# Expert stage: the third low part moves from Pool to VectorE, the output copy from VectorE to ACT

## The chip, the cores and the metric

The kernel runs on one core of a Trainium2 chip. The metric is device time in microseconds (us) of one execution. Three runs of the kernel before took 919.23, 915.85 and 917.68 us, median 917.68. The engines are TensorE (PE in the rows; its weight loads are PEld), VectorE (DVE), ScalarE (ACT), GpSimd (POOL) and SyncE (SP, here used only to issue transfers; its queue is SPq). They work side by side, each through its own instructions in order, and wait for each other by semaphores.

## What is computed

One encoder layer on 768 tokens of width 1024 (512 of one sequence, 256 of another), in float32. First a mixer (attention branches with a gated sum), then a mixture of experts, then a last norm. The change touches only the experts:

```python
for e in range(N_EXPERTS):                       # 16 experts, D_EXPERT = 256
    he = jax.nn.silu(t @ w_exp_gate[e]) * (t @ w_exp_up[e])
    out = out + dense_w[:, e:e + 1] * (he @ w_exp_down[e]).astype(jnp.float32)
```

`dense_w` is nonzero for two experts of a token: it picks one of four groups, and the best two of the four experts in it.

## The kernel before, in words

Matmuls in full precision are made as three passes of rounded operands. Every operand is split into a high part (a copy rounded to the matmul's type) and a low part (the rest, operand minus high part); a product is high x high, high x low, low x high. So each expert weight goes through SBUF three times: raw as loaded, high, low.

The tokens are sorted by expert into tiles of 128 rows. In this execution there are 19 tiles, numbered from 0; three of them (13, 15 and 17) belong to the same expert as the tile before, so that 16 sets of weights are loaded. A set is three chunks of 128x2048 floats, 1024 KB each: chunk 0 (gate), 1 (up) and 2 (down). Raw chunks, high parts and low parts have two buffers each, by the tile's parity.

TensorE sets the order. For tile j it does, in `tile`: `turn_rows(j+1)`, eight transposes of the next tile's gathered rows; `gate_up(j)`, 24 matmuls; `down(j-1)`, 12 matmuls; `turn_hidden(j)`, two transposes of the hidden values. In the rows, L1102 is turn_rows, L1122 turn_hidden, and L831 to L833 are the three passes.

Around it, for tile j:

- SP loads the chunks 0 and 1 of tile j+4 and chunk 2 of tile j+3 (line 561) and stores the result of a finished tile (line 579). A raw buffer is loaded again when the low part of the tile two before it is made (`s_elo`).
- ACT makes the high parts: of the next rows (`xt_hi`, line 1396), the gate's tanh (1403), chunks 0 and 1 of tile j+2 (1318), the hidden values (`he_hi`, 1410), chunk 2 of tile j+1 (1318 again).
- DVE makes the low parts: of the next rows (`xt_lo`, 1818), the hidden product `he` in two steps (1828, 1830), chunks 0 and 1 of tile j+2 (1639); then it copies the output of tile j-1 out of PSUM (`y_sb`, 1843) and makes the hidden low part (`he_lo`, 1834).
- POOL gathers the rows of a tile from memory by an indirect transfer (724; inside the loop a small copy, 721, brings the indices ahead of it) and makes the low part of chunk 2 (733 and 739; 744 where the expert is the same as before).

Where a tile's expert is that of the tile before, the high and low parts are copied from the other buffer and nothing is loaded; a register and two branches decide that on each engine. Tiles 0 to 2 are written out; a hardware loop does two tiles in a round, and the last two are written out again.

Before the tiles start, SP issues chunk 2 of tiles 2 and 3 in this order, each of which waits for the low part of chunk 2 two tiles before it:

```python
            for j in (2, 3):
                load_expert(j, 0, j, 2)
            sp.wait_ge(s_fill, 16)
```

After this come chunks 0 and 1 of tile 4, and then the loop.

Of the kernel before, what the change touches and what calls it, by code (L numbers as in the profile page):

```python
# [28 lines left out]
ACT = mybir.ActivationFunctionType  # L29
ALU = mybir.AluOpType  # L30
AX = mybir.AxisListType

P = 128
# [23 lines left out]
SET = 3  # L57
# [152 lines left out]
def build(nc, x_prompt, x_sample, rel_bias, norm_mix, w_in, lam_q1, lam_k1, lam_q2, lam_k2, subln_g,  # L210
# [9 lines left out]
    with ctx:  # L220
# [8 lines left out]
        ones = misc("ones", [P, P])  # L229
# [79 lines left out]
        y_sb = at("y_sb", [P, 2, D], F32, A_OA + 24576)  # L309
# [168 lines left out]
        def over(ap, shape, dim):  # L478

            return ap.unsqueeze(dim).broadcast_to(shape)  # L480
# [14 lines left out]
        def late(r, j, first):  # L495

            return not isinstance(r, int) or j >= first

        def is_new(eng, r, j):

            return eng.value_load(regs[0:1, 2, bass.ds(r * 2 + j, 1)], min_val=0, max_val=1)
# [156 lines left out]
        def _(gp):  # L658
# [65 lines left out]
                gp.indirect_dma_start(xg[:, j % 2, :], None, h2_dram.ap(),  # L724
                                      bass.IndirectOffsetOnAxis(ap=ids, axis=0)).then_inc(s_xg[j % 2], 16)

            def split_lo_part(r, j, c):

                lo, hi = e_lo[j % 2][c], e_hi[j % 2][c]
                if not late(r, j, SET + 1):  # L730
                    gp.wait_ge(s_elo[c], r * 2 + j)
                    gp.wait_ge(s_ehi[c], r * 2 + (j + 1))
                    gp.tensor_tensor(lo, e_raw[j % 2][:, c, :], hi, ALU.subtract).then_inc(s_elo[c], 1)
                    return
                new = is_new(gp, r, j)
                with gp.If(new > 0):
                    gp.wait_ge(s_elo[c], r * 2 + j)
                    gp.wait_ge(s_ehi[c], r * 2 + (j + 1))
                    gp.tensor_tensor(lo, e_raw[j % 2][:, c, :], hi, ALU.subtract).then_inc(s_elo[c], 1)
                with gp.If(new < 1):  # L740
                    gp.wait_ge(s_elo[c], r * 2 + j)
                    gp.wait_ge(s_ehi[c], r * 2 + (j + 1))

                    gp.tensor_tensor(lo.rearrange("p (a b) -> p a b", b=P),
                                     e_lo[1 - j % 2][c].rearrange("p (a b) -> p a b", b=P),
                                     over(ones[:, :], [P, 16, P], 1), ALU.mult).then_inc(s_elo[c], 1)


            gp.wait_ge(s_tab, 1)
            for done in s_h2out:  # L750
                gp.wait_ge(done, 16 * (NT // 2))
            for j in range(3):
                gather(0, j)
            split_lo_part(0, 1, 2)

            loops = loop_count(gp)
            for j in (3, 4):
                gather(0, j)
            split_lo_part(0, 2, 2)
            with gp.Fori(0, loops) as r:  # L760
                for j in (3, 4):
                    gather(r, j + 2)
                    split_lo_part(r, j, 2)
            split_lo_part(loops, 3, 2)
            split_lo_part(loops, 4, 2)

            gp.wait_ge(s_ystored, 2)
            for t in range(NT):
# [391 lines left out]
        def _(act):  # L1160
# [141 lines left out]
            def split_expert(r, j, chunks):  # L1302

                par = j % 2
                new = is_new(act, r, j) if late(r, j, SET + 1) else None

                def free(c):


                    if c == 2 and late(r, j, 2):  # L1310
                        act.wait_ge(s_dn, r * 2 + (j - 1))

                def split(c):
                    free(c)
                    if late(r, j, SET + 1):
                        act.wait_ge(s_ehi[c], r * 2 + j)
                    act.wait_ge(s_eraw[c][par], r * 16 + 16 * (j // 2 + 1))
                    act.activation(e_hi[par][c], e_raw[par][:, c, :], ACT.Copy).then_inc(s_ehi[c], 1)  # L1318

                if not late(r, j, SET + 1):  # L1320
                    for c in chunks:
                        split(c)
                    return
                with act.If(new > 0):
                    for c in chunks:
                        split(c)
                with act.If(new < 1):
                    for c in chunks:
                        free(c)
                        act.wait_ge(s_ehi[c], r * 2 + j)  # L1330
                        act.activation(e_hi[par][c], e_hi[1 - par][c], ACT.Copy).then_inc(s_ehi[c], 1)
# [67 lines left out]
            def tanh_gate(r, j):  # L1399
                act.wait_ge(s_gu, r * 2 + (j + 1))  # L1400
                if late(r, j, 2):
                    act.wait_ge(s_he, r * 4 + 2 * (j - 1))
                act.activation(tanh_g[:, j % 2, :], main[0][:, 512 * (j % 2):512 * (j % 2) + DE], ACT.Tanh,
                               scale=0.5).then_inc(s_tanh, 1)

            def hidden_hi(r, j):
                act.wait_ge(s_htr, r * 2 + (j + 1))
                if late(r, j, 2):
                    act.wait_ge(s_dn, r * 2 + (j - 1))
                act.activation(he_hi[:, j % 2, :, :], work[1][:, 0:DE].rearrange("p (k n) -> p k n", k=2),  # L1410
                               ACT.Copy).then_inc(s_hehi, 1)

            def tile(r, j):
                rows_hi(r, j + 1)
                tanh_gate(r, j)

                split_expert(r, j + 2, (0, 1))
                hidden_hi(r, j)
                if late(r, j, 1):
                    split_expert(r, j + 1, (2,))  # L1420
# [7 lines left out]
                tile(r, 4)  # L1428
            rows_hi(loops, 4)
            tanh_gate(loops, 3)  # L1430
            hidden_hi(loops, 3)
            split_expert(loops, 4, (2,))
            tanh_gate(loops, 4)
            hidden_hi(loops, 4)

            for t in range(NT):
                act.wait_ge(s_comb, combined(t))
# [13 lines left out]
        def _(dve):  # L1451
# [380 lines left out]
            def hidden_lo(r, j):  # L1832
                dve.wait_ge(s_hehi, r * 2 + (j + 1))
                dve.tensor_tensor(he_lo[:, j % 2, :, :], work[1][:, 0:DE].rearrange("p (k n) -> p k n", k=2),
                                  he_hi[:, j % 2, :, :], ALU.subtract).then_inc(s_helo, 1)

            def copy_y(r, j):
                dve.wait_ge(s_dn, r * 2 + (j + 1))
                if not late(r, j, 1):
                    dve.wait_ge(s_fill, 16)  # L1840
                if late(r, j, 2):
                    dve.wait_ge(s_yout[j % 2], r * 16 + 16 * (j // 2))
                dve.tensor_copy(y_sb[:, j % 2, :], main[1][:, :]).then_inc(s_y, 1)

            def tile(r, j):
                rows_lo(r, j + 1)
                if not late(r, j, 1):
                    route_weights()
                hidden(r, j)
                split_expert(r, j + 2, (0, 1))  # L1850
                if late(r, j, 1):
                    copy_y(r, j - 1)
                hidden_lo(r, j)

            split_expert(0, 1, (0, 1))
            rows_lo(0, 0)
# [6 lines left out]
                tile(r, 4)  # L1863
            rows_lo(loops, 4)
            hidden(loops, 3)
            copy_y(loops, 2)
            hidden_lo(loops, 3)
            hidden(loops, 4)
            copy_y(loops, 3)
            hidden_lo(loops, 4)  # L1870
            copy_y(loops, 4)


            def finish(t):
# [82 lines left out]
```

## Time and profile before

| | before |
|---|---|
| median of 3 runs | 917.68 us (915.85 to 919.23) |
| profiled execution | 918.5 us, its span 916.7 us |
| PE busy | 842.0 us (92%) |
| DVE busy | 465.3 us (51%) |
| ACT busy | 392.3 us (43%) |
| POOL busy | 191.2 us (21%) |
| granted TensorE clock over the span | 0.972 of full speed |

The expert stage lies at about 680 to 876 us of the span. Busy shares over the whole span hide it, since the mixer before it uses the engines otherwise. A row of the timeline gives an instruction's start, its duration, its engine and line, and in brackets how long the engine had stood idle before it and what ended that. Starts can lie some 0.1 us before the end of the instruction ahead, as engines overlap them.

### The profile page before, as it was taken

The numbers are of one execution on the slowest core, as the hardware profiler recorded it, in microseconds if no ns is written. First come the engines' busy times: TensorE is split into PE (matmuls) and PEld (weight loads), VectorE is DVE, ScalarE is ACT, GpSimd is POOL, SyncE is SP. The second block draws the span as 40 slices with busy tenths as digits, with TensorE's granted clock in tenths as the row PEclk, the third lists the DMA queues.
The fourth block names the chain that finished last, engine by engine and source line by source line (L and its number), as shares of the span: only waits on it lengthen the run. The fifth ranks groups of instructions, "written<-read, shape, count | busy, mean of one in ns | idle before, by whom it ended". The sixth has DMA issues, their size and how long they took to land.

```text
span 916.7 us, 13495 instructions
## 1 busy us (share of the span) xinstructions
PE 842.0 (92%) x5122; PEld 719.6 (79%) x5122; DVE 465.3 (51%) x760; ACT 392.3 (43%) x540; POOL 191.2 (21%) x132
## 2 busy tenths in 40 slices
PE   3999999999999999999999999999989998989910
PEld 3988888998788888888888888888977876878700
DVE  4511354454419632333233147434598877777537
ACT  5522244444432543334333202234426866767413
POOL 0001010000000001100100001300024778767553
PEclk9999999999999999999999999999899999999965
DMA  9315131322121314321311114873869999988675
GB/s 290 88 56 122 47 75 46 76 67 55 36 76 34 93 46 75 87 58 46 76 47 46 46 46 154 244 324 129 308 207 324 370 375 381 390 284 276 230 278 207
DMA packets 97355, 142.46 MB, mean 155 GB/s; under 512 B 4567, under 2 KB 75431, under 8 KB 97223
## 3 DMA queue, kind: packets, MB, share of 16 engines
q1 hardware_dynamic: 89368, 115.05, 37.2%
q0 software_dynamic: 7904, 26.44, 10.6%
q8 instruction: 36, 0.59, 0.3%
q10 hardware_dynamic: 32, 0.26, 0.3%
q14 instruction: 15, 0.11, 0.0%
HBM read 116.31 MB, written 25.43 MB: 155 GB/s over the span
## 4 chain that ended last, share of the span: by engine, by line
PE 77%; DVE 7%; SPq 6%; DMA 4%; issue 3%; ACT 2%; POOL 1%; ACTq 0%; DVEq 0%; POOLq 0%
PE main L831 20%; PE main L833 19%; PE main L832 19%; PE work L910 3%; SPq L579 3%; PE work L880 2%; PE work L943 2%; PE work L927 2%; PE work L1071 1%; SPq L561 1%; PE work L1049 1%; DVE x L1891 1%; PE work L897 1%; DMA raw<-in_w_in 1%; DMA xg<-h_rows,column 1%
## 5 line engine op out<-in xcount | busy, mean ns | idle before, releaser
L831 PE MATMUL main<-ht_hi,w_hi 128*128 128x512 f32 (+1 forms) x576 | 198.5, 345 | 0.0
L832 PE MATMUL main<-ht_lo,w_hi 128*128 128x512 f32 (+1 forms) x576 | 194.1, 337 | 0.0
L833 PE MATMUL main<-ht_hi,w_lo 128*128 128x512 f32 (+1 forms) x576 | 194.0, 337 | 0.0
L1462 DVE TENSOR_TENSOR w_lo<-raw,w_hi 128x2048 fp32r<-128x2048 f32 x30 | 68.7, 2290 | 236.7 <-ACT w_hi L1170 236.7
L831 PEld LDWEIGHTS main<-ht_hi,w_hi 128*128 128x128 f32 x576 | 109.3, 190 | 18.6 <-issue 5.2
L833 PEld LDWEIGHTS main<-ht_hi,w_lo 128*128 128x128 f32 x576 | 109.2, 190 | 11.8
L832 PEld LDWEIGHTS main<-ht_lo,w_hi 128*128 128x128 f32 x576 | 109.4, 190 | 11.0
L831 PE MATMUL main<-w_hi,ht_hi 128*128 128x256 f32 (+1 forms) x304 | 96.5, 318 | 3.4 <-DVE ht_lo L1479 3.4
L680 POOL DMA_DIRECT2D bias<-bias_vectors x16 | 12.4, 774 | 413.7 <-DVE nmx L1522 176.4
L833 PE MATMUL main<-w_hi,ht_lo 128*128 128x256 f32 (+1 forms) x304 | 93.6, 308 | 0.0
L832 PE MATMUL main<-w_lo,ht_hi 128*128 128x256 f32 (+1 forms) x304 | 93.6, 308 | 0.0
L1639 DVE TENSOR_TENSOR e_lo<-e_raw,e_hi 128x2048 fp32r<-128x2048 f32 x32 | 73.6, 2333 | 19.2 <-ACT e_hi L1318 19.2
L1318 ACT ACTIVATE e_hi<-e_raw 128x2048 fp32r<-128x2048 f32 x38 | 71.5, 1910 | 21.6 <-DMA e_raw<-in_w_exp_down 12.4
L1170 ACT ACTIVATE w_hi<-raw 128x2048 fp32r<-128x2048 f32 x30 | 57.2, 1908 | 25.4 <-PE main L833 24.3
L831 PEld LDWEIGHTS main<-w_hi,ht_hi 128*128 128x128 f32 x304 | 58.9, 194 | 11.2 <-issue 8.3
L831 PE MATMUL main<-e_hi,xt_hi 128*128 128x512 f32 x152 | 61.6, 405 | 0.0
L833 PEld LDWEIGHTS main<-w_hi,ht_lo 128*128 128x128 f32 x304 | 58.8, 193 | 2.6
L832 PEld LDWEIGHTS main<-w_lo,ht_hi 128*128 128x128 f32 x304 | 58.9, 194 | 2.1
L832 PE MATMUL main<-e_lo,xt_hi 128*128 128x512 f32 x152 | 60.1, 395 | 0.0
L833 PE MATMUL main<-e_hi,xt_lo 128*128 128x512 f32 x152 | 59.9, 394 | 0.0
L1213 ACT ACTIVATE prob<-prob,nmx 128x512 f32<-128x512 f32 (+1 forms) x48 | 30.7, 641 | 40.6 <-DVE nmx L1515 40.6
L1246 ACT ACTIVATE blk<-main 128x768 f32<-128x768 f32 x16 | 13.0, 811 | 74.3 <-PE main L833 74.3
(265 smaller groups left out, 1533.1 us busy)
## 6 DMA issues: line engine op xcount, KB each, us to landing
e_raw<-in_w_exp_gate SPq DMA_DIRECT2D x16, 1024.0 KB, 8.6
e_raw<-in_w_exp_up SPq DMA_DIRECT2D x16, 1024.0 KB, 10.3
e_raw<-in_w_exp_down SPq DMA_DIRECT2D x16, 1024.0 KB, 8.3
raw<-in_w_in SPq DMA_DIRECT2D x28, 512.0 KB, 5.0
expert_rows<-y_sb SPq DMA_DIRECT2D x19, 512.0 KB, 9.9
raw<-in_w_in SPq DMA_DIRECT2D x9, 1024.0 KB, 5.0
expert_rows<-y_sb SPq DMA_DIRECT2D x1, 5632.0 KB, 22.4
raw<-in_w_out SPq DMA_DIRECT2D x4, 1024.0 KB, 5.4
```

The costliest lines, as they stand in the source:

```text
L579: sp.dma_start(y_rows[:, bass.ds(r * 2 + j, 1) if not isinstance(r, int) else slice(j, j + 1), :], y_sb[:, j % 2:j % 2 + 1, :]).then_inc(s ...
L831: pe.matmul(out, s_hi, m_hi, start=(first and i == 0), stop=False)
L832: pe.matmul(out, s_hi, m_lo, start=False, stop=False)
L833: last = pe.matmul(out, s_lo, m_hi, start=False, stop=(final and i == n - 1))
L880: last = pe.matmul(ps[:, at0:at0 + S], query_columns(blk[rows, DIFF_Q[h], :], t), blk[rows, DIFF_K[h], s0:s0 + S], start=True, stop=True)
L910: last = pe.transpose(ps[:, P * i:P * i + P], prob[:, u % 2, c:c + P], ident[:, :])
L927: last = pe.matmul(ps[:, 0:P], v, prob_t[:, u % 2, P * i:P * i + P], start=(i == 0), stop=(i == n - 1))
L1170: act.activation(w_hi[:, c % 2, :], raw[:, c % 2, :], ACT.Copy).then_inc(s_whi, 1)
L1213: last = act.activation(pr, pr, ACT.Exp, bias=nmx[:, i, c:c + 1], accum_out=den[:, i, c:c + 1])
L1318: act.activation(e_hi[par][c], e_raw[par][:, c, :], ACT.Copy).then_inc(s_ehi[c], 1)
L1462: dve.tensor_tensor(w_lo[:, c % 2, :], raw[:, c % 2, :], w_hi[:, c % 2, :], ALU.subtract).then_inc(s_wlo, 1)
L1639: dve.tensor_tensor(e_lo[par][c], e_raw[par][:, c, :], e_hi[par][c], ALU.subtract).then_inc(s_elo[c], 1)
```

## The change

POOL keeps the gathers and loses all its arithmetic in this stage. DVE makes the low part of chunk 2 as it makes the other two, as the last step of its tile, for tile j+1. The copy of tile j-1's output out of PSUM leaves DVE and goes to ACT, between the high parts of chunks 0 and 1 and the hidden high part.

```diff
@@ POOL
-            split_lo_part(0, 1, 2)
             loops = loop_count(gp)
             for j in (3, 4):
                 gather(0, j)
-            split_lo_part(0, 2, 2)
             with gp.Fori(0, loops) as r:
                 for j in (3, 4):
                     gather(r, j + 2)
-                    split_lo_part(r, j, 2)
-            split_lo_part(loops, 3, 2)
-            split_lo_part(loops, 4, 2)
@@ ACT
+            def copy_y(r, j):
+                act.wait_ge(s_dn, r * 2 + (j + 1))
...
+                act.activation(y_sb[:, j % 2, :], main[1][:, :], ACT.Copy).then_inc(s_y, 1)
             def tile(r, j):
                 rows_hi(r, j + 1)
                 tanh_gate(r, j)
                 split_expert(r, j + 2, (0, 1))
+                if late(r, j, 1):
+                    copy_y(r, j - 1)
                 hidden_hi(r, j)
                 if late(r, j, 1):
                     split_expert(r, j + 1, (2,))
@@ DVE
             def tile(r, j):
                 rows_lo(r, j + 1)
...
                 hidden(r, j)
                 split_expert(r, j + 2, (0, 1))
-                if late(r, j, 1):
-                    copy_y(r, j - 1)
                 hidden_lo(r, j)
+                split_expert(r, j + 1, (2,))
```

What each engine does where the prediction looks. On DVE, before, tile 0 (after its hidden product) and the first steps of tile 1 (`e_lo_82` and `e_lo_86` are the buffers of even and odd tiles):

```order
L1639 TENSOR_TENSOR e_lo_82<-e_raw_87,e_hi_81 128x2048 x2
L1834 TENSOR_TENSOR he_lo<-work,he_hi 128x256
L1818 TENSOR_TENSOR xt_lo<-work,xt_hi 128x1024
L1828 SCALAR_TENSOR_TENSOR he<-tanh_g,main 128x256
L1830 SCALAR_TENSOR_TENSOR he<-he,main 128x256
L1639 TENSOR_TENSOR e_lo_86<-e_raw_88,e_hi_85 128x2048 x2
L1843 COPY y_sb<-main 128x1024
L1834 TENSOR_TENSOR he_lo<-work,he_hi 128x256
```

The same place on DVE after the change:

```order
L1625 TENSOR_TENSOR e_lo_82<-e_raw_87,e_hi_81 128x2048 x2
L1820 TENSOR_TENSOR he_lo<-work,he_hi 128x256
L1625 TENSOR_TENSOR e_lo_86<-e_raw_88,e_hi_85 128x2048
L1804 TENSOR_TENSOR xt_lo<-work,xt_hi 128x1024
L1814 SCALAR_TENSOR_TENSOR he<-tanh_g,main 128x256
L1816 SCALAR_TENSOR_TENSOR he<-he,main 128x256
L1625 TENSOR_TENSOR e_lo_86<-e_raw_88,e_hi_85 128x2048 x2
L1820 TENSOR_TENSOR he_lo<-work,he_hi 128x256
```

The single `e_lo_86` (chunk 2 of tile 1) now stands behind the hidden low part of tile 0 and ahead of the next `xt_lo`; `y_sb` is gone.

On POOL, before, the start of the expert stage (`table_u` holds the indices of all tiles; `e_lo0d` is the even tiles' chunk 2):

```order
L724 DMA xg<-h_rows,table_u 128x1024 x3
L733 TENSOR_TENSOR e_lo_86<-e_raw_88,e_hi_85 128x2048
L505 TENSOR_LOAD regs
L505 ISA x2
L724 DMA xg<-h_rows,table_u 128x1024 x2
L733 TENSOR_TENSOR e_lo0d<-e_raw_87,e_hi0d 128x2048
```

The same place on POOL after the change:

```order
L724 DMA xg<-h_rows,table_u 128x1024 x3
L505 TENSOR_LOAD regs
L505 ISA x2
L724 DMA xg<-h_rows,table_u 128x1024 x2
L736 UNCONDITIONAL_BRANCH
L736 ISA
```

The low parts of chunk 2 of tiles 1 and 2, which stood between the gathers, are gone, and the gathers follow each other.

## Rows read from the trace of the kernel before

**Rows 1.** Waits of PE in the expert stage: us in total, times, longest us.
```profile
PE work L1102 <- DMA xg<-h_rows,column: 6.6, 5, 2.8
PE main L831 <- DVE he_lo L1834: 1.9, 3, 1.4
```
**Rows 2.** Timeline of PE: hidden turns of tiles 0, 10, 11, 12, 17 and a gather's wait.
```profile
691.46 0.44 PE L1122 MATMUL work<-ident,he 128*128 128x128 f32 x2 [1.79 <-DVE he L1830]
...
792.10 0.38 PE L1122 MATMUL work<-ident,he 128*128 128x128 f32 x2
...
801.87 0.38 PE L1122 MATMUL work<-ident,he 128*128 128x128 f32 x2
805.01 1.09 PE L1102 MATMUL work<-ident,xg 128*128 128x128 f32 x8 [2.76 <-DMA xg<-h_rows,column]
814.13 0.38 PE L1122 MATMUL work<-ident,he 128*128 128x128 f32 x2
...
860.71 0.38 PE L1122 MATMUL work<-ident,he 128*128 128x128 f32 x2
```
**Rows 3.** Timeline of POOL: low part of chunk 2, index copy, gather.
```profile
685.24 4.60 POOL L733 TENSOR_TENSOR e_lo<-e_raw,e_hi 128x2048 fp32r<-128x2048 f32 x1 [2.07 <-DVE e_lo0d L1639]
...
759.70 2.26 POOL L721 COPY column<-table_u 128x1 uint32 x1
...
788.00 4.63 POOL L739 TENSOR_TENSOR e_lo0d<-e_raw,e_hi0d 128x2048 fp32r<-128x2048 f32 x1 [4.43 <-ACT e_hi0d L1318]
...
795.61 2.67 POOL L724 DMA_INDIRECT xg<-h_rows,column  x1 [0.79 <-POOL column L721]
```
**Rows 4.** Stretches: us, busy by engine, PEclk, DMA share of 16 engines, GB/s.
```profile
688.00:700.00 12.00, 10.21 (x51) 8.29 (x50) 10.03 (x12) 6.88 (x7) 4.25 (x3) 1.00 0.97 355
700.00:712.00 12.00, 12.00 (x64) 10.02 (x63) 9.04 (x8) 8.78 (x8) 6.09 (x3) 1.00 0.95 300
...
742.00:797.00 55.00, 51.76 (x243) 42.20 (x242) 42.61 (x36) 36.41 (x31) 40.33 (x16) 0.97 1.06 384
```
**Rows 5.** DMA issues of the page: KB each, us to landing.
```profile
e_raw<-in_w_exp_down SPq DMA_DIRECT2D x16, 1024.0 KB, 8.3
```
**Rows 6.** Timeline of ACT: high parts of chunk 2 that waited for loads, then `xt_hi`.
```profile
742.12 1.92 ACT L1318 ACTIVATE e_hi0d<-e_raw 128x2048 fp32r<-128x2048 f32 x1 [0.81 <-DMA e_raw<-in_w_exp_down]
...
796.79 1.92 ACT L1318 ACTIVATE e_hi<-e_raw 128x2048 fp32r<-128x2048 f32 x1 [1.49 <-DMA e_raw<-in_w_exp_down]
798.62 1.00 ACT L1396 ACTIVATE xt_hi<-work 128x1024 fp32r<-128x1024 f32 x1
```
**Rows 7.** Timeline of DVE: tile 0's hidden low part, a low part of chunk 0, tile 10's end, casts.
```profile
696.33 0.41 DVE L1834 TENSOR_TENSOR he_lo<-work,he_hi 128x256 fp32r<-128x256 f32 x1
...
759.27 2.65 DVE L1639 TENSOR_TENSOR e_lo<-e_raw,e_hi 128x2048 fp32r<-128x2048 f32 x1 [1.32 <-ACT e_hi L1318]
...
797.34 1.22 DVE L1843 COPY y_sb<-main 128x1024 f32<-128x1024 f32 x1
...
799.65 1.23 DVE L1818 TENSOR_TENSOR xt_lo<-work,xt_hi 128x1024 fp32r<-128x1024 f32 x1 [0.76 <-ACT xt_hi L1396]
800.79 0.41 DVE L1828 SCALAR_TENSOR_TENSOR he<-tanh_g,main 128x256 f32<-128x256 f32 x1
...
802.26 3.43 DVE L1652 CAST e_lo<-e_lo 128x2048 fp32r<-128x2048 f32 x2 [0.61 <-issue]
```
**Rows 8.** Low parts on DVE, by form: duration ns min/median/max, first and last start us.
```profile
L1639 DVE TENSOR_TENSOR e_lo<-e_raw,e_hi x32: 2279/2292/3281, 626.3 to 853.9; 128x2048 fp32r<-128x2048 f32 x32
L1652 DVE CAST e_lo<-e_lo x6: 1212/1348/2292, 802.3 to 843.1; 128x2048 fp32r<-128x2048 f32 x6
```
**Rows 9.** Timeline of SP's queue: chunk 2 of tiles 2 and 3, chunk 0 of tiles 4 and 5.
```profile
685.18 5.05 SPq L561 DMA_DIRECT2D e_raw<-in_w_exp_down  x2
694.39 0.39 SPq L561 DMA_DIRECT2D e_raw<-in_w_exp_gate  x1
...
702.98 0.38 SPq L561 DMA_DIRECT2D e_raw<-in_w_exp_gate  x1
```

More of the change, by code:

```diff
@@ L725, in gather @@
                                       bass.IndirectOffsetOnAxis(ap=ids, axis=0)).then_inc(s_xg[j % 2], 16)
[L727 to L746, printed above, removed]
             gp.wait_ge(s_tab, 1)
@@ L1411, in hidden_hi @@
                                ACT.Copy).then_inc(s_hehi, 1)
+            def copy_y(r, j):
+                act.wait_ge(s_dn, r * 2 + (j + 1))
+                if not late(r, j, 1):
+                    act.wait_ge(s_fill, 16)
+                if late(r, j, 2):
+                    act.wait_ge(s_yout[j % 2], r * 16 + 16 * (j // 2))
+                act.activation(y_sb[:, j % 2, :], main[1][:, :], ACT.Copy).then_inc(s_y, 1)
             def tile(r, j):
@@ L1430, in _ @@
             tanh_gate(loops, 3)
+            copy_y(loops, 2)
             hidden_hi(loops, 3)
@@ L1433, in _ @@
             tanh_gate(loops, 4)
+            copy_y(loops, 3)
             hidden_hi(loops, 4)
+            copy_y(loops, 4)
             for t in range(NT):
@@ L1835, in hidden_lo @@
                                   he_hi[:, j % 2, :, :], ALU.subtract).then_inc(s_helo, 1)
[L1837 to L1843, printed above, removed]
             def tile(r, j):
@@ L1865, in _ @@
             hidden(loops, 3)
-            copy_y(loops, 2)
             hidden_lo(loops, 3)
+            split_expert(loops, 4, (2,))
             hidden(loops, 4)
-            copy_y(loops, 3)
             hidden_lo(loops, 4)
-            copy_y(loops, 4)
             def finish(t):
```

## The prediction

> **What bounds the kernel now.** I read the waits of TensorE in the expert stage first, since the page's busy share (92%) is mixed with the mixer before it. TensorE waits there mainly for gathered rows, 6.6 us in five waits, the longest 2.8 [rows 1]. This is what the change is aimed at: POOL works in order, so a gather stands behind a low part, which stands behind an ACT high part, which stands behind a load. The reader can follow one instance: POOL waits 4.43 us for the high part, works 4.63 on the low part, and issues tile 13's gather only at 795.61 [rows 3]; it is used at 805.01, after 2.76 us of waiting [rows 2].
>
> Second, TensorE's pace. A tile takes 9.32 us where nothing waits ((860.71 - 814.13) / 5), and from tile 0 to 17 it took 860.71 - 691.46 = 169.25 us, 10.8 more than 17 x 9.32 [rows 2]. So 10.8 us is all that could come back in this part.
>
> Third, and against the change, the transfers. Between 742 and 797 the 16 DMA engines are full (share 1.06) at 384 GB/s [rows 4]. In that stretch ACT has to wait for every chunk 2: there are six such high parts, the first at 742.12, the last at 796.79, so (796.79 - 742.12) / 5 = 10.93 us apart [rows 6]. A tile moves three chunks of 1024 KB [rows 5], a gather and a store of 512 KB each (128x1024 floats): 4.19 MB, and 4.19 MB / 10.93 us = 384 GB/s. The two views agree: the transfers deliver a tile every 10.93 us, and TensorE, which could do one in 9.32, lives in this stretch from the lead it had. By tile 11 the lead is used up. The load of its chunk 2 lets ACT start at 796.79; `xt_hi` follows, then DVE's `xt_lo` at 799.65, the two `he` steps from 800.79 [rows 6, 7], and turn_hidden(11) starts at 801.87 [rows 2]: 5.08 us from load to TensorE, with no slack left on this path. The earlier gather waits are thus covered by the loads, and only the one behind tile 11 is paid: tile 12 takes 814.13 - 801.87 = 12.26 us, 2.94 over 9.32.
>
> After tile 12 three of the tiles load nothing, and TensorE sets the pace again at 9.32 us.
>
> **The change part by part.**
>
> POOL's low parts go, and its gathers follow as soon as their buffer is free. The wait before tile 12 goes: **-2.9 us**. Bounds: 0 (gathers still late) and -10.8 (every lost time of rows 2).
>
> The third low part comes onto DVE, 2.29 us [rows 8], between `he_lo` and `xt_lo`. On the path from load to TensorE it takes the place of `xt_hi` (1.00 [rows 6]), which now runs beside it: 1.92 + 2.29 + 1.23 + 0.41 + 0.42, about 6.3 instead of 5.08. **+1.2 us**, once, as the loads keep their distance. Bounds 0 and 2.3. DVE's tile becomes 3 x 2.29 + 1.23 + 0.41 + 2 x 0.41 = 9.3 us [rows 7, 8] and up to 0.6 where a branch isn't hidden (0.61 before a cast [rows 7]): 9.3 to 9.9, about TensorE's 9.32. While the loads take 10.93 that is covered; without this cover it costs up to 0.6 us a tile. In the last tiles half of the low parts are casts of 1.35 instead of 2.29 [rows 8], so DVE stays below 9.32.
>
> `y_sb` leaves DVE (1.22 [rows 7]) for ACT, at some 1.0 us like `xt_hi`, which also empties 128x1024 from PSUM. ACT stood waiting for loads by 0.81 to 1.49 us in the rows shown [rows 6], and this wait hides it; where it doesn't, ACT and with it the path grow by up to 1.0. For the last tile the copy is itself on the path, with the last hidden high part behind the copy ahead of it: -0.2 and +0.1, **-0.1 us**.
>
> The start is where I see the price. SP issues chunk 2 of tile 3 only when chunk 2 of tile 1 has its low part. POOL made that at 685.24 to 689.84 [rows 3]; SP's second issue ends at 685.18 + 5.05 = 690.23 [rows 9]. Now it stands on DVE behind tile 0's hidden low part (696.33 + 0.41 [rows 7]), so it is done near 699.0, 9.2 us later. SP's queue behind it holds chunks 0 and 1 of tile 4 (first issued at 694.39 [rows 9]); they wait as well. So 3.15 MB move from about 690 to about 699, in front of the stretch that is full. From 688 to 700 the transfers moved 355 x 12 = 4.26 MB [rows 4]. With the three chunks held back, what is left to move there is the rest of the chunk issued at 685.18 and what was under way with it (1.3 MB, estimated) and two gathers (1.05): 1.9 MB are missing at 700. From 700 to 712 only 300 of 384 GB/s were used [rows 4], so up to 1.0 MB can be caught up, of which I take 0.75, as the first data come some time after the issue. 1.15 MB stay missing, at 384 GB/s **+3.0 us** on every later load. Bounds: 0 (all caught up) and 9.2 (nothing).
>
> The gathers come one tile sooner, so one more gather (0.52 MB) is in front of the weights of tile 11: 0.52 / 384 GB/s, **+1.4 us**. Bounds 0 and 1.4.
>
> Sum: -2.9 + 1.2 - 0.1 + 3.0 + 1.4 = **+2.6 us**: turn_hidden(11) some 5.6 us later than 801.87, tile 12 only 2.6 later, and the same pace behind it. On the profiled execution's 918.5 us this is 921.1. That execution lies 0.8 over the median of the runs, so for the median 917.68 + 2.6 = 920.3 us.
>
> **The rivals.**
>
> *The loads don't bind, and TensorE gets its time back.* For it: all large waits of TensorE name the gather [rows 1]. Against it: ACT's six waits and the full DMA engines [rows 4, 6]. Then 10.8 us come back, less what DVE's 9.3 to 9.9 takes in some nine tiles with three full low parts (0.2 each, near the lower end: 2 us): -9, 909 us. 17%.
>
> *The loads bind, but nothing of the start is lost,* since the queue holds enough to catch up: -2.9 + 1.2 - 0.1, and 0 to 1.4 for the gather: about -1, 916.5 us. For it: the 300 GB/s from 700 to 712. 13%.
>
> *Slower: SP's queue passes its delay on.* Place: the second chunk 2 issue, with two chunks behind it. If the loads are full from 699 on and nothing is caught up, 1.9 MB cost 4.9 instead of 3.0, and with the whole 9.2 us passed on the sum is +8.8; midway, with ACT's copy not hidden (+1.0), some +7, 924.5 us. It decides once more than 1.9 MB are missing when the full stretch begins. For it: from 742 on there is no free transfer time at all [rows 4]. Against it: the slack at 700 to 712. 20%.
>
> *POOL stays late.* At 759.70 POOL's index copy took 2.26 us and ended at 761.96, just when DVE's low part of 759.27 ended (761.92) [rows 3, 7]. With a third low part on DVE it can happen more often. A gather's way to its use, 9.4 us from issue at 795.61 to 805.01 [rows 2, 3], has two tiles (18.6 us) once it isn't queued behind arithmetic, so about 8 us are free for such holds, against 2 x 2.3 if both copy and gather are held. If they are late all the same, the 2.9 stays: +5.5, 923.2 us. 5%. The Trainium skill (SBUF — State Buffer, section "SBUF: two separate sides") says that VectorE and GpSimd have one pair of ports in common, which an operation of VectorE with two SBUF inputs holds alone against a GpSimd operation that reads SBUF. By that rule the third low part adds a hold in every tile; these two rows agree with it, and the holds would fit into the 8 us.
>
> **How the numbers follow.** My forecast, 920.3 us, has 45%; its own range, from the bounds of the start (0.75 MB more or less caught up) and the branches, is 917.5 to 924. Changes under 0.5%, 4.6 us, can hardly be told from none with this kernel. Faster by more: the first rival but for its smaller gains, 15%. Slower by more: most of the third and fourth rival and the upper end of the forecast, 29%. The rest, 56%, lies between. The range takes in a part of the first rival and most of the third: 911 to 926 us.
>
> **What would show it.** Right: in the profile after, SP's second chunk 2 issue ends near 699 instead of 690.2; the GB/s of 688 to 700 fall to some 200; no wait of TensorE for gathered rows is left; TensorE waits instead for `he`, which stands behind DVE's third low part; tiles 6 to 11 come some 10.9 us apart; ACT's six waits for chunk 2 stand 4 to 5 us later. POOL is busy only with gathers and copies. Wrong: if the tiles 6 to 11 come nearer than 10.5 us, the transfers were no bound, and the first rival is right; if the chunk 2 loads land no later than before, the start cost nothing; if waits for gathered rows remain, POOL is held by DVE.

## The result, and the profile after

The changed kernel takes 921.38 us, median of 5 runs (920.77 to 922.76), against 917.68 (5 runs, 915.02 to 919.23): ratio 1.0064, interval 1.0045 to 1.0082. It is slower, as was forecast (920.3). By how much is less sure: the ratio on record is above that of the two medians (1.0040), and the kernel before, whose runs lie between 913.5 and 920.7, had medians of 916.21, 916.45 and 916.74 in the later experiments (21 to 28 runs each), so 917.68 is a high one. The profiled execution took 921.38 us with a span of 919.5.

TensorE's waits in the expert stage, after (columns as in [rows 1]):

```profile
PE work L1095 <- DVE he L1816: 9.6, 8, 1.5
```

The gather of [rows 1] is gone from the list; TensorE now waits for `he`, the product that stands on DVE behind the third low part. The hidden turns of tiles 0, 10, 11, 12 and 17, after:

```profile
689.92 0.44 PE L1095 MATMUL work<-ident,he 128*128 128x128 f32 x2 [1.45 <-DVE he L1816]
...
794.67 0.44 PE L1095 MATMUL work<-ident,he 128*128 128x128 f32 x2 [1.52 <-DVE he L1816]
...
805.98 0.38 PE L1095 MATMUL work<-ident,he 128*128 128x128 f32 x2
...
815.49 0.44 PE L1095 MATMUL work<-ident,he 128*128 128x128 f32 x2
...
863.50 0.38 PE L1095 MATMUL work<-ident,he 128*128 128x128 f32 x2
```

In this execution tile 0 comes 1.54 us earlier than in the one of before, since the work ahead of the expert stage ran a little faster: 0.7 us of the shift stand already at 626 us. So I count everything from turn_hidden(0). Then tile 11 is 5.65 us later than in [rows 2] (116.06 against 110.41), tile 12 2.90, tile 17 4.33, and from there to the end nothing changes. 4.33 - 1.54 is the 2.8 us between the spans.

SP's queue, after: start, duration of the issue, and what it issues:

```profile
684.01 14.13 SPq L561 DMA_DIRECT2D e_raw<-in_w_exp_down  x2
700.42 0.39 SPq L561 DMA_DIRECT2D e_raw<-in_w_exp_gate  x1
```

The second chunk 2 issue ends at 698.14 instead of 690.23 [rows 9], and chunk 0 of tile 4 follows at 700.42 instead of 694.39. The transfers, after (columns as in [rows 4]), and below them one row of before that is not in [rows 4]:

```profile
688.00:700.00 12.00, 10.25 (x52) 8.05 (x51) 10.09 (x10) 8.43 (x8) 1.81 (x1) 1.00 0.52 174
700.00:712.00 12.00, 11.70 (x62) 9.76 (x61) 10.78 (x8) 7.80 (x8) 3.72 (x3) 1.00 1.04 365
712.00:742.00 30.00, 28.43 (x138) 22.92 (x138) 26.43 (x21) 25.54 (x23) 8.35 (x6) 1.00 1.06 383
742.00:797.00 55.00, 48.03 (x228) 38.48 (x227) 45.34 (x36) 39.74 (x35) 17.07 (x11) 0.99 1.06 381
```

```profile
712.00:742.00 30.00, 29.12 (x142) 23.73 (x141) 25.32 (x23) 22.13 (x20) 23.13 (x9) 1.00 1.03 369
```

From 688 to 700 the transfers lose (355 - 174) x 12 = 2.2 MB, from 700 to 712 they catch up (365 - 300) x 12 = 0.8 MB, from 712 to 742 another (383 - 369) x 30 = 0.4 MB, and from 742 on they are as full as before. ACT's waits for chunk 2 of tiles 6 and 11 (answering to [rows 6]):

```profile
744.49 1.92 ACT L1291 ACTIVATE e_hi0d<-e_raw 128x2048 fp32r<-128x2048 f32 x1 [1.68 <-DMA e_raw<-in_w_exp_down]
...
799.26 1.92 ACT L1291 ACTIVATE e_hi<-e_raw 128x2048 fp32r<-128x2048 f32 x1 [0.52 <-DMA e_raw<-in_w_exp_down]
```

From one such wait to the next it is again (799.26 - 744.49) / 5 = 10.95 us. Ahead of these six there are now two more, at 722.61 and 733.53: ACT waits for loads from tile 4 on instead of tile 6. Counted from turn_hidden(0), the last one, chunk 2 of tile 11, starts at 109.34 instead of 105.33. I call this number the **load time** below: it tells how late the transfers are at the end of the full stretch. DVE behind it (answering to [rows 7]):

```profile
801.28 2.29 DVE L1625 TENSOR_TENSOR e_lo<-e_raw,e_hi 128x2048 fp32r<-128x2048 f32 x1 [1.00 <-ACT e_hi L1291]
803.49 1.22 DVE L1804 TENSOR_TENSOR xt_lo<-work,xt_hi 128x1024 fp32r<-128x1024 f32 x1
804.62 0.41 DVE L1814 SCALAR_TENSOR_TENSOR he<-tanh_g,main 128x256 f32<-128x256 f32 x1
805.07 0.42 DVE L1816 SCALAR_TENSOR_TENSOR he<-he,main 128x256 f32<-128x256 f32 x1
```

This is the longer path from load to TensorE: 805.49 - 799.26 = 6.23 us to the end of `he`, against 5.08 in all before. turn_hidden(11) starts another 0.49 later, because TensorE is itself late here: after its wait of 1.52 us the granted clock fell. Stretch, its length, PE busy, granted clock, DMA share, GB/s:

```profile
792.00:794.00 2.00, 1.15 (x6) 1.00 1.07 401
794.00:800.00 6.00, 5.20 (x20) 0.72 1.03 419
```

0.72 is a mixture of the levels 1.2 and 2.4 GHz in the six us behind the wait. Behind the waits of 1.45 and 1.40 us in tiles 6 and 8 the granted clock stayed at 1.00, so what made it fall here is open.

One thing I had not priced stands in the last tiles. They come 9.51 and 9.70 to 9.72 us apart in turn instead of 9.32. ACT, then DVE, then TensorE around turn_hidden(14), after:

```profile
823.65 3.72 ACT L1304 ACTIVATE e_hi<-e_hi 128x2048 fp32r<-128x2048 f32 x2 [0.49 <-issue]
827.27 1.00 ACT L1392 ACTIVATE y_sb<-main 128x1024 f32<-128x1024 f32 x1
828.17 0.38 ACT L1383 ACTIVATE he_hi<-work 128x256 fp32r<-128x256 f32 x1
828.43 1.92 ACT L1291 ACTIVATE e_hi0d<-e_raw 128x2048 fp32r<-128x2048 f32 x1
```

```profile
830.46 2.29 DVE L1625 TENSOR_TENSOR e_lo0d<-e_raw,e_hi0d 128x2048 fp32r<-128x2048 f32 x1 [1.45 <-ACT e_hi0d L1291]
832.66 1.22 DVE L1804 TENSOR_TENSOR xt_lo<-work,xt_hi 128x1024 fp32r<-128x1024 f32 x1
...
834.24 0.42 DVE L1816 SCALAR_TENSOR_TENSOR he<-he,main 128x256 f32<-128x256 f32 x1
```

```profile
834.72 0.44 PE L1095 MATMUL work<-ident,he 128*128 128x128 f32 x2
835.28 1.09 PE L1075 MATMUL work<-ident,xg 128*128 128x128 f32 x8
```

No load is waited for here, and DVE is idle for 1.45 us. The chain runs through both engines in order: ACT's copies of two high parts (the expert is repeated), its output copy, its hidden high part, its high part of chunk 2, and only then DVE's low part and `he`, which ends at 834.66, when TensorE has been ready for a moment. The copy of 1.00 us is a link of that chain.

### The profile page after: what moved, and what is told of

It is laid out like the page before. It is cut to its first block, busy times and chain, and to the rows that moved or that the text cites. A ratio compares the mean times of both kernels' runs of the same rounds, so it can differ in the third digit from the quotient of the medians.

```text
span 919.5 us, 13458 instructions
## 1 busy us (share of the span) xinstructions
PE 841.6 (92%) x5122; PEld 716.7 (78%) x5122; DVE 474.4 (52%) x759; ACT 409.6 (45%) x559; POOL 110.6 (12%) x113
## 4 chain that ended last, share of the span: by engine, by line
PE 75%; DVE 8%; SPq 7%; issue 3%; DMA 3%; ACT 2%; POOL 0%; ACTq 0%; DVEq 0%
PE main L804 20%; PE main L805 19%; PE main L806 19%; SPq L579 4%; PE work L883 3%; PE work L853 2%; SPq L561 2%; PE work L916 2%; PE work L900 2%; DVE e_lo L1625 1%; DVE x L1866 1%; PE work L870 1%; PE work L1022 1%; DMA raw<-in_w_in 1%; DMA e_raw<-in_w_exp_down 1%
## 5 line engine op out<-in xcount | busy, mean ns | idle before, releaser
L1625 DVE TENSOR_TENSOR e_lo<-e_raw,e_hi 128x2048 fp32r<-128x2048 f32 x38 | 86.1, 2289 | 14.0 <-ACT e_hi L1291 10.9
```

What stands on the lines that cost most here:

```text
L1625: dve.tensor_tensor(e_lo[par][c], e_raw[par][:, c, :], e_hi[par][c], ALU.subtract).then_inc(s_elo[c], 1)
```

## The experiments

Each ratio is to the kernel before on the same chip; as its median differs from one experiment to the next, ratios are set side by side below, and not times. The load time, the path (load time to turn_hidden(11)) and the stretch from turn_hidden(11) to turn_hidden(17) are read from each trace as above, in us:

| kernel | ratio, interval | load time | path | tiles 11 to 17 |
|---|---|---|---|---|
| before | 1 | 105.33 | 5.08 | 58.84 |
| after | 1.0064 (1.0045-1.0082) | 109.34 | 6.72 | 57.52 |
| e1 | 1.0004 (0.9991-1.0016) | 104.64 | 6.28 | 56.90 |
| e2 | 1.0043 (1.0026-1.006) | 108.17 | 6.26 | 55.86 |
| e3 | 1.0075 (1.0057-1.0093) | 103.80 | 8.58 | 61.15 |
| e4 | 0.997 (0.9957-0.9983) | no wait | | 58.63 |
| e5 | 1.0033 (1.0019-1.0047) | 109.41 | 4.93 | 56.37 |
| e7 | 0.9989 (0.9975-1.0004) | 105.29 | 4.92 | 56.37 |
| e8 | 1.0043 (1.0027-1.0058) | 109.46 | 6.29 | 56.16 |
| e10 | 0.9993 (0.9978-1.0008) | 105.36 | 6.29 | 55.83 |
| e12 | 1.0011 (0.9998-1.0024) | 105.85 | 6.28 | 56.94 |
| e13 | 1.0003 (0.9989-1.0016) | 105.48 | 5.85 | 56.38 |

The last three columns come from one execution of each kernel, so small differences between two of them say little. In e2 and e3 TensorE comes late to tile 11 from waits for gathered rows, so their path is not that of the loads; in e2 `he` ends 5.19 us after the load time, 4.86 in the kernel before.

### e1: tile 1's low part early again

One instruction of the change goes back to where POOL had it in time; the edit is in DVE's `tile`, against the changed kernel.

```diff
                     route_weights()
+                    split_expert(r, j + 1, (2,))
                 hidden(r, j)
...
-                split_expert(r, j + 1, (2,))
+                if late(r, j, 1):
+                    split_expert(r, j + 1, (2,))
```

> The kernel after, with one step moved: DVE makes the low part of chunk 2 of tile 1 in tile 0 ahead of the hidden product, where it stood idle 2.5 us for the first tanh, and not behind the hidden low part. Transfers theory (the loads bind in tiles 6 to 11, and the three chunks held back at the start are the largest cost): SP's second chunk 2 issue ends near 688.5 instead of 698.1, the GB/s of 688 to 700 return to about 350, the six chunk 2 landings come some 3 us sooner, and the time falls by about 3.0 us to 918.4. VectorE theory (its third low part sets the pace, the start is made up for later): the landings may move, the time stays within 0.5 us of 921.4.

Measured 916.96 us, ratio 1.0004. The 918.4 expected on 917.68 is a ratio of 1.0008, inside the interval; the rival's 921.4 is 1.004, outside it. SP's queue, and ACT's chunk 2 of tile 11:

```profile
685.50 5.16 SPq L561 DMA_DIRECT2D e_raw<-in_w_exp_down  x2
```

```profile
796.00 1.92 ACT L1291 ACTIVATE e_hi<-e_raw 128x2048 fp32r<-128x2048 f32 x1 [1.12 <-DMA e_raw<-in_w_exp_down]
```

SP's second issue ends at 690.66, near that of [rows 9] and not at the 688.5 expected, and the load time falls from 109.34 to 104.64. One instruction of 2.29 us, moved in the order, holds nearly the whole loss of the change: 4.7 us of load time, more than the 3 us I gave it.

### e2: only that low part late, all else as before

The edit is against the kernel before: one line of POOL, two at the end of DVE's `tile`.

```diff
-            split_lo_part(0, 1, 2)
...
+                if not late(r, j, 1):
+                    split_expert(r, j + 1, (2,))
```

> The kernel before, with one step moved: the low part of chunk 2 of tile 1 alone goes from POOL to DVE, behind tile 0's hidden low part; all other low parts stay on POOL and the output copy on DVE. Transfers theory: SP holds the three chunks back as in the kernel after, every later landing comes about 3 us later, and as the path from load to TensorE had no slack at tile 11, the time rises by about 3.0 us to 920.7. VectorE theory: one more low part of 2.3 us in tile 0 is absorbed, the time stays at 917.7, at most 0.5 more.

Measured 920.91 us, ratio 1.0043 (2.4 to 5.5 us slower): slower, as the theory had it. ACT's chunk 2 of tile 11, with turn_hidden(0) at 691.23:

```profile
799.40 1.92 ACT L1317 ACTIVATE e_hi<-e_raw 128x2048 fp32r<-128x2048 f32 x1 [1.50 <-DMA e_raw<-in_w_exp_down]
```

Load time 108.17, so +2.84 against before, where +3.0 was forecast. The delay of one early issue is a loss by itself. The traced execution does not hold all of it: its turn_hidden(17) is only 1.04 later than before, counted from turn_hidden(0), since TensorE no longer waits for tile 13's gather (tiles 11 to 17 take 55.86 instead of 58.84). So the rise by the ratio is more than this trace explains. It was one of e2's faster executions (919.38); that of the kernel before (918.5) lies above its median.

### e12: the late low part kept, SP's order changed

The edit is in SP's program, against the changed kernel.

```diff
-            for j in (2, 3):
-                load_expert(j, 0, j, 2)
+            load_expert(2, 0, 2, 2)
             sp.wait_ge(s_fill, 16)
...
             load_tile(0, 4, (0, 1))
+            load_expert(3, 0, 3, 2)
```

> The changed kernel, but SP issues chunks 0 and 1 of tile 4 ahead of chunk 2 of tile 3, so that only this one chunk waits for VectorE's late low part of tile 1. Theory (the start's cost is the transfers that stand in SP's queue behind the waiting issue): chunks 0 and 1 of tile 4 are issued near 694 and 696 again; at 700 one chunk of 1.05 MB is missing instead of 1.9 MB and 0.75 of it is caught up, so ACT's chunk 2 of tile 11 starts some 106 us after turn_hidden(0) instead of 109.3, and the time is about 3 us less: ratio 1.003. Rival (the late low part costs by itself, whatever stands behind it in the queue): 109.3 and 1.006 as in the changed kernel.

Measured 917.3 us, ratio 1.0011. SP's queue, the transfers, and ACT's chunk 2 of tile 11 (turn_hidden(0) is at 690.24):

```profile
693.50 0.39 SPq L561 DMA_DIRECT2D e_raw<-in_w_exp_gate  x1
695.56 0.38 SPq L561 DMA_DIRECT2D e_raw<-in_w_exp_up  x1
698.09 0.38 SPq L561 DMA_DIRECT2D e_raw<-in_w_exp_down  x1
```

```profile
688.00:700.00 12.00, 10.29 (x50) 8.05 (x48) 9.77 (x10) 8.11 (x8) 1.80 (x1) 1.00 0.73 266
700.00:712.00 12.00, 11.51 (x60) 9.67 (x61) 11.02 (x9) 9.58 (x9) 3.44 (x3) 1.00 1.07 370
```

```profile
796.09 1.92 ACT L1291 ACTIVATE e_hi<-e_raw 128x2048 fp32r<-128x2048 f32 x1 [0.49 <-DMA e_raw<-in_w_exp_down]
```

Load time 105.85, where 106 was expected; the ratio is lower than the 1.003 expected. 3.5 us of the delay are given back although the low part is as late as in the change. So it is mainly the two chunks behind the waiting issue in SP's queue that cost. The chunk that still waits leaves 1.2 us against e1's 104.64.

### e4: half of chunk 1 loaded from tile 4 on

This kernel leaves out half of the up weights' transfer; the rest of the buffer keeps old data. The edit is in SP's `load_expert`, against the changed kernel.

```diff
-                sp.dma_start(put(e_raw[j % 2][:, c, :]), expert_v[c][e]).then_inc(s_eraw[c][j % 2], 16)
+                dst, src = put(e_raw[j % 2][:, c, :]), expert_v[c][e]
+                if c == 1 and late(r, j, 4):
+                    dst, src = dst[:, 0:4, :], src[:, 0:4, :]
+                sp.dma_start(dst, src).then_inc(s_eraw[c][j % 2], 16)
```

> The kernel after, but from tile 4 on only half of chunk 1 (the up weights) is loaded, so that a tile moves 3.67 instead of 4.19 MB; the other half keeps old data, so these experts' outputs are not the reference's. No engine's work changes. Transfers theory: tiles 6 to 11 come 3.67 MB / 384 GB/s = 9.6 us apart instead of 10.95, or DVE's 9.5 to 9.9 where that is more; at tile 11 some 6 us are gained, and the time falls to about 915. VectorE theory: the pace of 10.95 stays, the time stays at 921.

Measured 912.91 us, ratio 0.997; the 915 expected on 917.68 is the same ratio. Its transfers from 742 to 797, columns as in [rows 4]:

```profile
742.00:797.00 55.00, 54.31 (x264) 43.99 (x263) 50.70 (x42) 45.48 (x40) 18.72 (x11) 1.00 1.01 363
```

ACT waits for no load in this stretch, and tiles 4 to 10 come 9.45 to 9.74 apart instead of the 10.9 to 11.0 from tile 5 on in the change. With fewer bytes the pace comes back, on the same engines with the same work: the transfers were the bound. The next bound is about 9.6 us a tile, 9.5 and 9.7 in turn as in the last tiles of the change. In its own last tiles e4 is slower than the change (58.63): ACT's output copy there waits twice for TensorE, 4.6 us in all, and TensorE then waits for `he` behind it.

### e3: only the output copy moves to ACT, POOL keeps its low parts

Against the kernel before; first ACT's `tile`, then DVE's. The helper and the copies of the last tiles, which are written out, move along (not shown).

```diff
                 split_expert(r, j + 2, (0, 1))
+                if late(r, j, 1):
+                    copy_y(r, j - 1)
                 hidden_hi(r, j)
...
                 split_expert(r, j + 2, (0, 1))
-                if late(r, j, 1):
-                    copy_y(r, j - 1)
                 hidden_lo(r, j)
```

> The kernel before, with only the output copy moved from DVE to ACT; POOL keeps its low parts. Transfers theory: nothing on the path from load to TensorE changes (copy was not on it), gathers stay late, the time stays within 1 us of 917.7. VectorE theory: DVE is 1.2 us shorter in every tile, so some nine tiles gain up to 1.2 us each and the time falls clearly, to 912 or less. If ACT's copy is not hidden in ACT's waits, up to 1 us a tile is lost where TensorE sets the pace, six tiles: up to 923.

Measured 923.21 us, ratio 1.0075. The time expected, within 1 us of the kernel before, was missed, and the VectorE theory's gain too. The price named for a copy that isn't hidden, 923 on 917.68 or a ratio of 1.006, was reached and passed, but by another cause than the one expected. POOL:

```profile
770.28 0.19 POOL L721 COPY column<-table_u 128x1 uint32 x1
...
788.34 4.62 POOL L739 TENSOR_TENSOR e_lo0d<-e_raw,e_hi0d 128x2048 fp32r<-128x2048 f32 x1
792.90 2.26 POOL L721 COPY column<-table_u 128x1 uint32 x1
795.95 2.23 POOL L724 DMA_INDIRECT xg<-h_rows,column  x1 [0.79 <-POOL column L721]
798.20 4.61 POOL L739 TENSOR_TENSOR e_lo<-e_raw,e_hi 128x2048 fp32r<-128x2048 f32 x1
```

POOL is without a break here: from 788.34 to 798.20 it needs 9.86 us for a tile, more than TensorE's 9.32. TensorE waits 11.0 us for gathered rows, in five waits, although the loads come earlier than before (103.80). The index copy took 0.19 us at 770.28, when DVE made no low part, and 2.26 at 792.90, beside one of 792.17. With DVE freed of the output copy the two meet more often: six index copies between 720 and 815 us took 2.24 to 2.28 us, three in the kernel before. The Trainium skill (SBUF — State Buffer, section "SBUF: two separate sides") says that VectorE's operations with two SBUF inputs and GpSimd's reads of SBUF share a pair of ports that one of them holds alone; the 2.26 beside a low part, which takes 2.29 by itself, agrees with it. The two halves of the change are no sum: the copy alone hurts through POOL, which the other half empties.

### e8: POOL's low parts to DVE, the copy stays on DVE

Against the changed kernel; first ACT's `tile`, then DVE's. Helper and last tiles again move along (not shown).

```diff
-                if late(r, j, 1):
-                    copy_y(r, j - 1)
                 hidden_hi(r, j)
...
+                if late(r, j, 1):
+                    copy_y(r, j - 1)
                 hidden_lo(r, j)
```

> Only the Pool part of the change: VectorE makes all three low parts and keeps the copy of the outputs. VectorE's tile is then 3 x 2.29 + 1.23 + 1.22 + 0.41 + 0.83 = 10.6 us and some branches, under the loads' 10.93 but over TensorE's 9.32. Theory (ACT's copy costs the last tiles some 1.4 us in the changed kernel, since it is in the chain ACT to VectorE; VectorE as a bound costs more): the last six tiles are some 10.0 to 10.8 apart where nothing is repeated, the time is 925 to 928 us, ratio 1.009 to 1.012. Rival (the copy's place is indifferent, the start's delay is the whole cost): ratio 1.005 to 1.0065.

Measured 920.58 us, ratio 1.0043: the theory's 925 to 928 is refuted; the rival's 1.005 to 1.0065 is not, by the time alone. DVE's tile is 10.6 us as worked out (its low parts of chunk 2 start at 759.94 and 770.53).

That is just under the loads' 10.95, so the load time is as in the change (109.46). In the last tiles I had forgotten the casts: every second expert there is repeated, and the tiles come 9.35 to 9.37 apart. The trace speaks against the rival: the copy on ACT costs 57.52 - 56.16 = 1.4 us more there than on DVE; the intervals of the two ratios overlap.

### e10: early low part, and ACT's copy at the end of its tile

The edit is in ACT's `tile`, against e1.

```diff
-                if late(r, j, 1):
-                    copy_y(r, j - 1)
                 hidden_hi(r, j)
                 if late(r, j, 1):
                     split_expert(r, j + 1, (2,))
+                    copy_y(r, j - 1)
```

> The changed kernel with tile 1's low part of chunk 2 made ahead of the first hidden product, and ACT's copy of the outputs moved from ahead of the hidden high part to the end of ACT's tile, behind the high part of chunk 2. Theory (ACT's copy, 1.0 us, lies in the chain ACT high part of chunk 2 to VectorE's low part to the next hidden product, and costs 1.4 us in the last tiles): the last tiles are 9.3 apart, ratio 0.9985 to 0.9995. Rival (the copy is hidden): ratio 1.0004 as with the early low part alone; if TensorE comes to wait for the copy to free the output's PSUM, above that.

Measured 916.24 us, ratio 0.9993; against e1 this is within the intervals. The trace is clear, at turn_hidden(13) and (14):

```profile
821.21 0.38 PE L1095 MATMUL work<-ident,he 128*128 128x128 f32 x2
830.51 0.38 PE L1095 MATMUL work<-ident,he 128*128 128x128 f32 x2
```

9.30 apart, and no slower one among the last five: tiles 11 to 17 take 55.83 instead of 56.90. The copy was in the chain. Of the 1.1 us gained in these tiles, 0.7 are lost again by a later load time.

### e5 and e7: the low part of chunk 2 behind the tile's own hidden product

The edit is in DVE's `tile`, against the changed kernel, with one line more in the written-out last tiles (not shown). e7 makes tile 1's low part early besides, as e1 does.

```diff
                 hidden(r, j)
+                if late(r, j, 2):
+                    split_expert(r, j, (2,))
                 split_expert(r, j + 2, (0, 1))
                 hidden_lo(r, j)
-                split_expert(r, j + 1, (2,))
+                if not late(r, j, 1):
+                    split_expert(r, j + 1, (2,))
```

> The changed kernel, but VectorE makes the low part of chunk 2 of a tile behind its own hidden product and no longer ahead of the next rows' low part (from tile 2 on; tile 1's stays where the change put it). Theory (the third low part stands in the path from a load, or from ACT's chain, to the next hidden product): turn_hidden(11) comes about 1.2 us earlier after tile 0 than in the changed kernel, the last tiles are 9.3 to 9.4 apart instead of 9.5 to 9.7, and the time is 2.0 to 2.6 us less than the changed kernel's: ratio to the kernel before 1.0035 to 1.0045. Rival (VectorE's total work counts, its place does not): the ratio stays at 1.006 to 1.007.

> As the run before (low part of chunk 2 behind the tile's own hidden product), with tile 1's low part made ahead of the first hidden product too, so that SP's second issue of chunk 2 is not held. Theory: the start's cost and the path's cost both go; 2 to 2.6 us less than the run with the early low part alone (ratio 1.0004): ratio 0.9975 (0.9965 to 0.999), SP's issue ends near 690. Rival (the place of the low part does not matter): 1.0004, as with the early low part alone.

e5 measured 919.63 us, ratio 1.0033; e7 915.71, ratio 0.9989. DVE in e5 behind chunk 2 of tile 11, whose load time is that of the change:

```profile
801.84 1.23 DVE L1804 TENSOR_TENSOR xt_lo<-work,xt_hi 128x1024 fp32r<-128x1024 f32 x1 [1.43 <-ACT xt_hi L1369]
```

The low part no longer stands ahead of `xt_lo`, and the path is 4.93 instead of 6.72 (6.28 at full clock). The path term is shown, with 1.35 against the 1.2 forecast. The last tiles gain 1.15. e7 ends at 0.9989, the upper end of what was expected, since its load time is 0.65 later than e1's.

### e13: all three

e7 with the copy's place of e10.

> The best of the earlier runs together: tile 1's low part early, the low part of chunk 2 behind the tile's own hidden product, and ACT's copy of the outputs at the end of ACT's tile. Theory: the last tiles are 9.3 apart instead of 9.3 to 9.47, the hidden low part no longer waits for the copy; the path from load to TensorE stays 4.9: ratio 0.9983 (0.997 to 0.9995). Rival (what is left is set by the loads and these reorderings only trade waits): 0.9989 as without the copy's move, or above.

Measured 916.78 us, ratio 1.0003: the theory missed, the rival held. TensorE's largest wait there:

```profile
PE main L804 <- ACT y_sb L1392: 5.2, 6, 1.3
```

The copy at the end of ACT's tile frees the output's PSUM too late for TensorE. And the path is 5.85 instead of 4.9, since the copy now stands between the load's high part (795.38) and `xt_hi` (798.11):

```profile
797.21 1.00 ACT L1392 ACTIVATE y_sb<-main 128x1024 f32<-128x1024 f32 x1
```

In e10 the same place costs nothing on the path, since DVE's low part runs beside it. The three reorderings trade one wait for another. No version was shown to beat the kernel before while computing the same: the lowest, e7, has an interval from 0.9975 to 1.0004.

### e6: gathers one tile later

The edit is in POOL's `gather`, against the changed kernel.

```diff
+                if not isinstance(r, int):
+                    gp.wait_ge(s_htr, r * 2 + (j - 2))
```

> The changed kernel with the gathers of the loop held back until the hidden turn of the tile three before, so that each stands about one tile later among the transfers. Theory (a gather made one tile sooner puts 0.52 MB ahead of the weights, +1.4 us): ACT's chunk 2 of tile 11 starts 1.4 us sooner after turn_hidden(0) than in the changed kernel, at about 107.9 instead of 109.3. Rival (the gather's place does not move the loads): 109.3. TensorE may come to wait for gathered rows here, so the time itself tells less: 919 to 924.

Measured 936.13 us (two runs), ratio 1.0218, above the 919 to 924 expected. TensorE waits:

```profile
PE work L1077 <- DMA xg<-h_rows,column: 20.6, 9, 4.4
```

The gathers became the bound, ACT no longer waits for loads, and so the load time says nothing: inconclusive on the question that it was made for.

## Why the prediction was right, and where not

| term | forecast | in the trace, from turn_hidden(0) | set apart by |
|---|---|---|---|
| wait for tile 13's gather, in tile 12 | -2.9 | 9.51 instead of 12.26: -2.75 | |
| loads later: start | +3.0 | +2.84 (in e2, alone) | e2; e1, e12 |
| loads later: one more gather ahead | +1.4 | +1.17 (the change against e2) | not by a run of its own |
| longer path from load to TensorE | +1.2 | +1.64, of it 0.44 clock | e5, e7 |
| last tiles | 0 | +1.43 | e5, e8, e10 |
| last copy | -0.1 | 0.0 | |
| sum | +2.6 | +4.3 | |

*What binds.* Right. e4 shows it: with fewer bytes the tiles come 9.45 to 9.74 apart. The first rival, 909 us, is refuted by that and by the tiles 6 to 11 of the change, 10.92 to 11.31 apart.

*The loads: the start and the gather ahead.* Together +4.4 was forecast, and +4.0 stands in the trace. At the start 2.2 MB were missing at 700 instead of 1.9; e12 shows that it is SP's queue, since with the two other chunks ahead of the waiting issue most of the loss goes. How the 4.0 splits can be read in the order of the prediction: e2 has the start's delay alone, +2.84, and the change adds 1.17 to it (e5 and e8, which are as late as the change, 1.24 and 1.29). The transfers agree. 105 us from turn_hidden(0) in the kernel before, e2, the change and e1, columns as in [rows 4]:

```profile
691.46:796.46 105.00, 100.88 (x485) 82.73 (x486) 83.22 (x71) 72.24 (x62) 70.47 (x28) 0.98 1.03 367
691.23:796.23 105.00, 96.62 (x462) 79.06 (x462) 84.12 (x71) 71.27 (x61) 70.72 (x28) 0.98 1.00 355
689.92:794.92 105.00, 96.00 (x462) 77.47 (x462) 89.93 (x70) 78.73 (x69) 30.91 (x19) 1.00 1.00 355
691.36:796.36 105.00, 99.69 (x486) 81.58 (x487) 92.15 (x72) 81.89 (x73) 33.28 (x21) 1.00 1.04 371
```

e2 and the change are both (367 - 355) x 105 us = 1.3 MB behind; 1.15 was forecast. What sets them apart is what was moved. The queue of the gathers from 660 us to the load time, packets, MB and share of the engines, before and after:

```profile
q0 software_dynamic: 1872, 6.82, 13.1%
q0 software_dynamic: 2016, 7.34, 13.8%
```

These are 13 and 14 gathers of 0.52 MB; e2 has 13, as the kernel before. So the change moves as much as e2, but one gather of 0.52 MB more ahead of tile 11's weights, as forecast.

Taken in the other order, the same 4.0 splits otherwise. e1, e7, e10 and e13 have the early gathers (7.34 MB) without the delay, and load times of 104.64 to 105.48 against 105.33 before: there the gather costs nothing against the kernel before, and the delay is worth 109.34 - 104.64 = 4.7. e1 moves (371 - 367) x 105 us = 0.4 MB more than the kernel before, most of it from 712 to 742 (385 GB/s instead of 369), so the gather found free transfer time there. In e2 the held chunks take that time (383 GB/s). The two prices are thus not independent, which the prediction had taken them to be: I had read only 742 to 797 and 700 to 712, and not the free time between. Its sum holds because in the change the delay leaves no free time for the gather. The kernel before is no clean base for this, though: e3, with its gathers as late as before, fills the same stretch (381 GB/s) and has a load time of 103.80, against which the four kernels are 0.8 to 1.7 later. The gather was not tested apart (e6 failed at it).

*The path.* Right: at full clock it is 6.28 to 6.29 in e1, e8, e10 and e12, which is the 1.2 over 5.08 that was forecast. The other 0.44 in the change came with the lower clock of that execution.

*The last tiles.* This term was missing. I had compared each engine's sum of work with 9.32, and DVE's was below it. The chain through ACT and DVE, which must run in order within one tile, is longer than either; ACT's copy, which its wait for loads was to hide, lies open where there are no loads to wait for. The prediction gave the price of that (up to 1.0 where the wait doesn't hide it), but put the last tiles at nothing, as DVE's sum stays below 9.32 there. Taking either link out of the chain shortens these tiles: the copy (e8, e10) or the low part (e5, e7). Per two tiles TensorE is 0.2 us late at one hidden turn and then loses about 0.35 more ahead of the next `turn_rows` (835.28 - 834.72 = 0.56 instead of 0.22).

*POOL.* No wait for gathered rows is left, so the fourth rival is refuted. The holds are still there, and fit. POOL, after:

```profile
785.13 1.30 POOL L721 COPY column<-table_u 128x1 uint32 x1 [6.24 <-PE work L1075]
787.22 2.21 POOL L724 DMA_INDIRECT xg<-h_rows,column  x1 [0.79 <-POOL column L721]
```

This gather, tile 13's, is used at 806.20, 19 us after its issue.

*ACT's six waits* were to stand 4 to 5 us later. They stand 2.4 to 2.5 later on the trace's time (744.49 and 799.26), and 3.9 to 4.0 from turn_hidden(0). That two more come ahead of them was not foreseen.

So the total came near mostly for the right reasons. turn_hidden(11) was to be 5.6 later and is 5.65 later from turn_hidden(0), tile 12 was to be 2.6 later and is 2.90; near as they are, the terms are partly off both ways (start and gather 0.4 less, the clock 0.44 more), and that is luck. What is short in the sum is the last tiles. Between the kernels 4.3 us stand in the trace, 3.7 between the medians, and 4.1 to 7.5 by the interval of the ratio, all above the forecast 2.6; that 920.3 lies as near to 921.38 as it does owes something to the high median of the kernel before.

## What to carry to other kernels

When a step moves later on an engine, look at which issue in a DMA queue waits for it, and count everything queued behind that issue: here the order of the queue was worth 3.5 of 4.7 us. An engine's sum of work below the pace isn't enough to call an instruction hidden; add up the chain that must run in order across engines within one tile, in each stage, and mind that what hides an instruction in one stage (a wait for loads) is missing in the next. Before charging a transfer that moves, read the free transfer time of all stretches up to the place where it is due, and mind that two delays can draw on the same free time.

## What the runs showed of the hardware

After a wait, TensorE lost more than the wait itself in these traces. After the change the next `turn_rows` follows a hidden turn by 0.28 us in tile 9 (783.64 to 783.92 in the trace), and by 0.57 in tile 10 (794.67 to 795.24); it is 0.27 to 0.28 in the tiles 5, 7 and 9, 0.56 to 0.61 in the tiles 6, 8, 10, 12 and 14, and 0.22 in the tiles 11, 13 and 15, where TensorE had not waited. In the kernel before, without such a wait, it is 0.22 in the even tiles 10, 12, 14 and 16 too. The loop of two tiles ends behind an even tile, so I take the 0.3 us for the loop's end, which is hidden as long as TensorE has work queued; that was not tested by itself.
